# Half of the first-key indicator tiles built on ScalarE, and 12 gather steps moved in among the lead builds

## The reference, cut to what matters

```
q = (xb @ w_q).reshape(blk, 8, 2, 128)                     # 8 heads, 2 half queries
sc = einsum('thpd,hpnd->thpn', q, sub_keys)                # scores against 128 keys each
top_s, top_i = top_k(sc, 16)
cand_s = top_s[:, :, 0, :, None] + top_s[:, :, 1, None, :]
cand_i = top_i[:, :, 0, :, None] * 128 + top_i[:, :, 1, None, :]
best_s, sel = top_k(cand_s.reshape(blk, 8, 256), 16)
gate = softmax(best_s); idx = cand_i at sel                # 16 of 16384 experts per head
act = gelu(einsum('thkd,td->thk', exp_u[idx], xb))
out = einsum('thk,thkd->td', gate * act, exp_v[idx])
```

## Time and profile before

| | |
|---|---|
| median of 3 runs | 3154.22 us |
| the profiled execution | 3153.1 us |
| its span | 3151.3 us |
| PE busy | 2943.6 us (93%) |
| DVE busy | 2475.3 us (79%) |
| ACT busy | 813.6 us (26%) |
| POOL busy | 1019.5 us (32%) |
| HBM read | 1033.28 MB |
| mean granted TensorE clock | 0.95 |

### The profile page before, as it was taken

How to read it: one execution, slowest core, us unless ns; L and a number is a source line. 1 busy time by engine, 2 the same in 40 slices (tenths; PEclk the granted TensorE clock), 3 DMA queues, 4 the chain that set the end, 5 groups by cost and what they waited for, 6 DMA issues and landing times.

```text
span 3151.3 us, 46747 instructions
## 1 busy us (share of the span) xinstructions
PE 2943.6 (93%) x17342; PEld 2573.4 (82%) x17342; DVE 2475.3 (79%) x5415; ACT 813.6 (26%) x2398; POOL 1019.5 (32%) x840
## 2 busy tenths in 40 slices
PE   8898999999999999987888979989999999999977
PEld 7797788988888888875766957779888888888865
DVE  2368899988888888887654787998888888888878
ACT  5332222221111212211355353222221122211212
POOL 5433222322233332333365321222333333333322
PEclk9799999999999999999988978989999999999989
DMA  5237788899999999999521356778999999999997
GB/s 185 83 100 294 271 316 321 341 421 422 422 421 422 421 415 420 421 407 419 222 80 54 100 201 266 285 298 307 420 422 421 422 421 420 421 416 417 412 422 292
DMA packets 159967, 1042.99 MB, mean 331 GB/s; under 512 B 18480, under 2 KB 23920, under 8 KB 44096
## 3 DMA queue, kind: packets, MB, share of 16 engines
q0 software_dynamic: 92160, 671.13, 52.2%
q1 hardware_dynamic: 63648, 357.59, 29.1%
q10 hardware_dynamic: 4000, 12.36, 1.0%
HBM read 1033.28 MB, written 7.86 MB: 330 GB/s over the span
## 4 chain that ended last, share of the span: by engine, by line
DMA 44%; PE 28%; DVE 18%; issue 8%; ACT 2%; DVEq 0%; POOL 0%; ACTq 0%; POOLq 0%
DMA gata<-uvg,idxg 37%; DVE acc L1657 8%; DMA gatb<-uvg,idxg 7%; PE bank L519 6%; PE bank L720 6%; PE bank L506 3%; PE bank L508 3%; PE bank L507 3%; PE bank L707 2%; DVE gata L1649 2%; PE bank L536 1%; PE bank L607 1%; PE bank L586 1%; DVE oneA L1623 1%; DVE rstd L1396 1%
## 5 line engine op out<-in xcount | busy, mean ns | idle before, releaser
L733 PE MATMUL bank<-a,V 128*128 128x256 f32 x4096 | 928.5, 386 | 59.9 <-DVE a L1640 47.1
L720 PE MATMUL bank<-xd,U 128*128 128x256 f32 x4096 | 939.1, 389 | 2.2 <-DMA U<-uvd 2.2
L733 PEld LDWEIGHTS bank<-a,V 128*128 128x128 f32 x4096 | 791.7, 194 | 180.2 <-issue 50.4
L1309 POOL DMA_INDIRECT gata<-uvg,idxg x428 | 499.0, 1166 | 1251.7 <-DVE acc L1657 1196.1
L720 PEld LDWEIGHTS bank<-xd,U 128*128 128x128 f32 x4096 | 789.7, 195 | 110.3 <-DMA U<-uvd 3.0
L1649 DVE CUSTOM_DVE_ANT_0 gata<-gata,xrow 128x1024 f32<-128x1024 f32 x428 | 522.1, 1220 | 219.5 <-DMA gata<-uvg,idxg 213.7
L1103 ACT ACTIVATE act<-dot 128x1 f32<-128x1 f32 x640 | 129.5, 202 | 1666.6 <-DVE dot L1649 1666.5
L1657 DVE SCALAR_TENSOR_TENSOR acc<-gata,wgt,acc 128x1024 f32<-128x1024 f32 x428 | 547.5, 1279 | 1.6 <-ACT wgt L1105 1.4
L1309 POOL DMA_INDIRECT gatb<-uvg,idxg x212 | 246.4, 1162 | 533.0 <-DVE acc L1657 523.3
L1649 DVE CUSTOM_DVE_ANT_0 gatb<-gatb,xrow 128x1024 f32<-128x1024 f32 x212 | 258.5, 1220 | 110.0 <-DMA gatb<-uvg,idxg 108.1
L707 PEld LDWEIGHTS bank<-B,oneA 128*128 128x128 f16 x4096 | 279.1, 150 | 29.1 <-issue 13.8
(11 more groups left out here) (198 smaller groups left out, 2519.0 us busy)
## 6 DMA issues: line engine op xcount, KB each, us to landing
U<-uvd SPq DMA_DIRECT2D x128, 1024.0 KB
V<-uvd SPq DMA_DIRECT2D x128, 1024.0 KB
raw<-lin SPq DMA_DIRECT2D x152, 512.0 KB
gata<-uvg,idxg POOLq DMA_INDIRECT x428
hsp<-h ACTq DMA_DIRECT2D x2, 2304.0 KB, 14.0
hx<-hsp SPq DMA_DIRECT2D x2, 2304.0 KB, 16.6
gatb<-uvg,idxg POOLq DMA_INDIRECT x212
sk_g<-skT ACTq DMA_DIRECT2D x2, 1024.0 KB, 4.8
```

The lines of the kernel that those rows point to most:

```text
L720: mm = pe.matmul(bank[s][:, TD * t:TD * t + TD], U[:, s, o:o + P], xd[:, k, :], start=(t == 0 and k == 0), stop=(k == DT - 1), skip_group_ ...
L733: mm = pe.matmul(bank[b][:, TD * (d % 2):TD * (d % 2) + TD], V[:, s, o:o + P], a[:, s, TD * k:TD * k + TD], start=(first and k == 0 and d ...
L1309: pool.indirect_dma_start(row(l, s), None, uvg[l], bass.IndirectOffsetOnAxis(idxg[:, s:s + 1], 0)).then_inc(g_in[s % SLOTS], 16)
```

## The change

Three things are changed.

First, ScalarE makes one of the two halves of oneA for the 17 lead builds, the second 8 tokens of each build. It takes for each token the absolute distance between the key numbers and the token's first key (a bias operand holds minus the key, one number per partition), 8 instructions of 128 elements with a stride, and then one instruction of 1024 elements, 1 - distance clipped at zero. VectorE makes only the first half for these builds; for later builds nothing changes.

Second, `gates_high` also writes minus the first keys, one more ScalarE instruction for each of two token chunks, ahead of the semaphore that VectorE's `take` waits for.

Third, the number of steps at the places of the lead rises: in layer 0 two at every place but those with m % 4 == 1 (30 steps, 8 more), in layer 1 two at every even m (26, 4 more). The tail then has 39 steps in layer 0 and 42 in layer 1.

```
-     ("sel3", 3), ("sel4", 3), *[(f"hot{m}", 1 + (m % 4 == 0)) for m in range(LEAD)]],
+     ("sel3", 3), ("sel4", 3), *[(f"hot{m}", 1 + (m % 4 != 1)) for m in range(LEAD)]],
...
-     ("sel2", 3), ("sel3", 3), ("sel4", 3), *[(f"hot{m}", 1 + (m % 4 == 0)) for m in range(LEAD)]])
+     ("sel2", 3), ("sel3", 3), ("sel4", 3), *[(f"hot{m}", 1 + (m % 2 == 0)) for m in range(LEAD)]])
...
-            def build(l, m, s):
+            def build(l, m, s, lead=False):
...
+                if lead:
+                    pe.wait_ge(a_act, LEAD * l + m + 1)
...
-                act.activation(gh[...], bank[b][:, 0:TCS[c]], ACT.Copy,
-                               scale=GS).then_inc(gh_done, 1)
+                act.activation(gh[...], bank[b][:, 0:TCS[c]], ACT.Copy, scale=GS)
+                act.activation(minus1[...], bank[b][:, P:P + TCS[c]], ACT.Copy,
+                               scale=-1.0).then_inc(gh_done, 1)
+
+            def ones_half(l, m):
+                s, t0 = m % 2, TB * (m % (TD // TB)) + TG
+                half = oneA[:, s, 1]
+                for t in range(TG):
+                    ins = act.activation(half[:, :, t], iotaA[:, :, t], ACT.Abs,
+                                         bias=minus1[:, t0 + t:t0 + t + 1])
+                ins.then_inc(a_dist, 1)
+                act.wait_ge(a_dist, LEAD * l + m + 1)
+                act.activation(half, half, ACT.Relu, bias=1.0, scale=-1.0).then_inc(a_act, 1)
...
                 n = max(n, RING0 - 1)
+                act.wait_ge(iota_in, 16)
+                act.wait_ge(gh_done, len(DC) * (l + 1))
+                ones_half(l, 0)
+                ones_half(l, 1)
                 weights_at(l, "hot0")
                 for m in range(1, LEAD):
                     weights_at(l, f"hot{m}")
                     to_w(l, m - 1)
+                    if m + 1 < LEAD:
+                        ones_half(l, m + 1)
                     if m % 2 == 1 and n + m // 2 < RING - 1:
                         gelu(l, n + m // 2)
...
-                for u in range(TB // TG):
+                for u in range(1 if m < LEAD else TB // TG):
                     ins = dve.tensor_tensor(oneA[:, s, u], iotaA[:, :, :], ...
```

More of the change, by code:

```diff
@@ L186, in program @@
         rstd = at_("rstd", 205312, [P, T], F32)
+        minus1 = at_("minus1", 205312, [P, TD], F32)
         ident = at_("ident", 207616, [P, P], F32)
@@ L292, in program @@
         a_one, b_eq, b_one = sem("a_one"), sem("b_eq"), sem("b_one")
+        a_dist, a_act = sem("a_dist"), sem("a_act")
         a_done, sums_done, hsum_done, dsum_done = (sem(n) for n in ("a_done", "sums_done", "hsum_done", "dsum_done"))
@@ L757, in experts @@
                 for m in range(LEAD):
-                    build(l, m, m % 2)
+                    build(l, m, m % 2, lead=True)
                     if m % 2 == 0 and n + m // 2 < RING:
@@ L1071, in gates_high @@
                 act.wait_ge(full[b], BASE[f"gt{l}"][b] + 1)
-                act.activation(gh[:, TCO[c]:TCO[c] + TCS[c]], bank[b][:, 0:TCS[c]], ACT.Copy,
-                               scale=GS).then_inc(gh_done, 1)
+                act.activation(gh[:, TCO[c]:TCO[c] + TCS[c]], bank[b][:, 0:TCS[c]], ACT.Copy, scale=GS)
+                act.activation(minus1[:, TCO[c]:TCO[c] + TCS[c]], bank[b][:, P:P + TCS[c]], ACT.Copy,
+                               scale=-1.0).then_inc(gh_done, 1)
[3 more added lines that the diff above has]
+                for t in range(TG):
+                    ins = act.activation(half[:, :, t], iotaA[:, :, t], ACT.Abs, bias=minus1[:, t0 + t:t0 + t + 1])
+                ins.then_inc(a_dist, 1)
+                act.wait_ge(a_dist, LEAD * l + m + 1)
+                act.activation(half, half, ACT.Relu, bias=1.0, scale=-1.0).then_inc(a_act, 1)
             def gate_exp(l, n):
```

## The result

| | before | changed |
|---|---|---|
| median of the runs, us | 3153.64 (4 runs, 3150.38 to 3160.45) | 3185.33 (4 runs, 3182.45 to 3193.81) |
| span of the profiled execution, us | 3151.3 | 3183.9 |
| mean granted clock | 0.95 | 0.944 |

The change makes the kernel slower: the ratio of the times is 1.0099, 95% interval 1.008 to 1.0119. The forecast was 3138.5 us; the time lies above its range of 3126 to 3158 us too.

The account below looks back on a forecast made before the run. It took PE to bound the loop and leads, bytes the tails, V's turnaround close behind. -26 + 2.5 + 0.5 + 6 + 0.5 + 1 = -15.5 us on 3153.1 gave 3137.6, predicted median 3138.5 us, range 3126 to 3158.

Parts of the forecast that it names:

- The tail loses steps: Tails: eight steps fewer in layer 0, four in layer 1, gaining 17 and 9 us, together 26 us.
- the second limit named: Tail: turnaround of V, close behind the bytes, 8.5 to 9.3 us an iteration, 136 to 149 us for 16.
- VectorE in the lead: Lead: 1.64 us left per build; four builds with 7 steps take 22.9 us, within PE's 23.9.
- ScalarE's half tile: Lead builds: eight short instructions at 0.31 us and a long one of 1.05, together 3.6 us, ends 2.8 and 4.2.
- The added wait and the start: Leads: builds wait for ScalarE, 2.5 and 0.5 us; late starts, 6 us in layer 0, 0.5 in layer 1.
- the chain through both engines: Lead: last dot, weight, `to_w`, half tile, 4.5 us before the next build; some 1.5 us more a pair if ScalarE bounds.
- DMA in the lead: Leads: layer 0 rises to 388 GB/s, layer 1 to some 355; fits on average, 1 us for missed bursts, bounds 0 and 5.
- The rival in which ScalarE becomes the bound: Leads: at 5.0 us a half tile, pairs take 13.3 us plus some 1.5, total 3180 us; chance 0.14.
- The point from which it decides the sign: Half tile price turning gain to loss: about 4.9 us without the chain's part, about 4.2 with it in full.
- The table loads: Rival: each lead build has two loads of 1.28 us on ScalarE, 72 us in all, about 3210 us; chance 0.03.

Follow-up runs that it names:

- dense_more: dense_early with four more steps in each lead (34 in layer 0, 30 in layer 1): 3127.88 us, 0.9914 of the kernel before.
- dense_half: Changed kernel with ScalarE's half tile laid out token by token, short instructions reading and writing adjacent numbers: 3122.9 us, 0.9899 of before; second series 3131.15 us, 0.9927.
- steps_only: Kernel before with only the 12 moved steps, VectorE making both halves of every tile: 3133.93 us, 0.9933 of before.
- write_dense: Changed kernel with the eight short instructions writing adjacent numbers, still reading with the 16-byte stride (second 8 tokens' indicator wrong): 3142.95 us, one run.
- dense_early: dense_half with the first two half tiles of a lead ahead of the still open gelu: 3122.37 us, 0.9908 of before; again 3123.7 us, 0.9896.
- write_gap4: Changed kernel with the eight short instructions writing every second 2-byte number, a 4-byte stride (second 8 tokens' indicator misordered): 3136.52 us, one run.
- half_only: Changed kernel with the steps back at their old places, ScalarE's half tile alone: 3202.5 us, 1.0148 of the kernel before.

## Why the prediction was wrong

**The tail loses steps.** Right in layer 0, little over half in layer 1. Forecast -17 and -9 us; measured -16.0 and -5.0, plus 3.9 us between the layers that the forecast did not count: layer 0's last steps end after its last sums, and fewer steps end sooner. VectorE's last two axpys there, before and changed:

```profile
1531.74 2.67 DVE L1657 SCALAR_TENSOR_TENSOR acc<-gata,wgt,acc 128x1024 f32<-128x1024 f32 x2
```

```profile
1544.44 2.67 DVE L1678 SCALAR_TENSOR_TENSOR acc<-gata,wgt,acc 128x1024 f32<-128x1024 f32 x2
```

From the last piece of scores to its end pass 168.7 us before and 149.4 changed: 19.3 of the 20 us that eight steps are by bytes, with DMA at 419 GB/s. So the bytes still set the pace there up to the last step. For the sums the second limit named, the wait for V, came forward. PE's waits in that tail, two rows before and the one row changed:

```profile
PE bank L733 <- DVE a L1640: 22.2, 9, 5.1
PE bank L733 <- DMA V<-uvd: 8.9, 3, 3.2
```

```profile
PE bank L737 <- DMA V<-uvd: 19.9, 8, 5.4
```

That V's turnaround bounds a tail by itself is shown by dense_more alone, where DMA falls to 385 GB/s. In layer 1 four steps by bytes are 10 us; dense_half and steps_only also had only 6 of them there. DMA is no longer full (403 GB/s), and PE waits 17.3 us for the gate product and 7.8 for V; why not more was gained was not settled.

**VectorE in the lead.** Right. A build is 1.64 us with one half (506.66 to 508.33 in the changed kernel's trace is 1.67), and in dense_half, where ScalarE keeps up, layer 0's lead is 97.5 us with 30 steps, as long as before with 22 (97.3). With both halves on VectorE the steps cost 8.6 us (steps_only), where the prediction had 6.4.

**ScalarE's half tile.** This is the step that failed. The sum took 3.6 us, with bounds of 2.8 and 4.2; measured 6.0. The row with a bias operand was the right one for the instruction but not for its addresses: it reads and writes adjacent 4-byte numbers. dense_half, with adjacent addresses, has 3.5 us. The prediction did name "strided 2-byte writes at half rate" and about 5 us, but outside its bounds and with no row. Against it it put `to_w`, as a strided write at 0.59 us. That was misread: in the lead `to_w` reads its bank with a stride (128 bytes) and writes its 512 4-byte numbers side by side (`Wr[:, i, :, :, :]`), so its row says nothing of strided writes.

**The added wait and the start.** PE did wait for ScalarE's half tile, as named, and the size followed the half tile. With 6.0 us a pair needs 2 x 6.0 + 3.3 = 15.3 us of ScalarE by the prediction's own count, measured 14.8 to 15.2. The extra 1.5 us a pair for the chain through both engines, which the prediction added on top, did not come with it; nor did its 2.5 and 0.5 us with dense_half, whose leads are 0.3 us longer and 2.3 us shorter than before. Build 0 of layer 0 was 6.7 us later (4.3 forecast), with the half tile of 3.5 us 4.8; the scores behind it took 9.02 us in place of 7.14 (1.5 us more were forecast). Build 0 of layer 1 was 2.5 us later, where 0.5 was forecast: ScalarE begins its half tile at 2104.87, 1.1 us behind the turn, and at 3.6 us the delay would be about nothing. In dense_half it is still 2.0 us late, since the half tile begins 3.1 us behind the turn, after a weight that waits for its dot and the copy of the key numbers (0.43 us).

**DMA in the lead.** Not reached with the change (302 GB/s). In dense_half the lead moved 380 GB/s with no longer lead, as forecast (388).

**The sum and the rivals.** The rival in which ScalarE becomes the bound came true. It was priced at 3180 us for 5.0 us a half tile, and given 0.14; the time is 3185 at 6.0. That the two are close is luck: by its own working 6.0 us would give 3212 us, and 3188 without the 1.5 us a pair for the chain, which did not come. The point from which it decides the sign (4.2 to 4.9 us) is in keeping with write_dense: 4.5 us a half tile, leads of 103.9 and 101.2, and a total still under the kernel before. Where its assumption on the half tile held, in dense_half, the sign and rough size came out: 3138.5 forecast, 3122.9 and 3131.15 measured, better by 7 to 16 us. In the traced execution (3130.87 us) the gain is 22.2 us against 15.5 forecast. The tails give 20.8 us in place of 26, the starts cost 6.8 (6.5 forecast), and the leads beyond them are 2.0 us shorter where 4 us of cost were forecast. What the sum left out gives 6.2 more: 4.0 between the layers and 4.1 ahead of the first lead and after the last tail, less 1.9 in the loops. The table loads did not appear: before and changed have 49 each, and abs and relu ran between gelus with none in the leads, as the Trainium skill, "ScalarE: Activation LUTs", section "Table sets: the hidden batching unit", says.

The same page's rule (section "Rules for kernel authors") that relu belongs on VectorE was right about the change: steps_only, which follows it, is 51 us faster in the medians. It is not borne out with the adjacent layout: dense_half is 11 us faster than steps_only in their comparison, and the lead of layer 0 with its start is 3.5 us shorter (4.8 later, 8.3 less), since in steps_only VectorE is the bound of that lead and ScalarE has the room. How much of the total it is worth stays open: dense_half's second series (0.9927 of before) lies beside steps_only's 0.9933, while dense_early's (0.9896, at most 0.9911) lies below it.

## What to carry to other kernels

When work goes to an idle engine, price it from a row that matches in addresses and element size, not only in operation and count; without such a row, keep the slow end inside the range and ask from which price the sign turns. Before giving up such a change, try the layout: the same work with adjacent addresses turned a loss of 1.0% into a gain of 0.7 to 1.0%. And try each half of a change alone: most of that gain, 0.7%, came from the moved steps with every tile left on VectorE. And moving transfers out of a full stretch pays only until the next limit behind it, here the two buffers of V at 141 to 142 us.

## What was not expected of the hardware

- ScalarE's 128-element activations from 2-byte to 2-byte numbers: 0.30 us from start to start with all addresses adjacent, 0.44 with the read 16 bytes apart, 0.62 with the write 16 bytes apart (whatever the read), 0.44 with the write 4 bytes apart and 0.46 with 4-byte numbers written 16 bytes apart, both with the read 16 bytes apart.
- A mean duration can mislead where instructions overlap: 1061 ns each, at 0.62 us from one start to the next.
- Equal work took different times. The turn ahead of layer 0's lead, before which nothing differs, ended at 479.5 us in write_gap4 and at 487.4 in half_only. In the window from 100 to 200 us the kernel before (shown first; half_only has the same 0.88) and write_gap4 had granted clocks of 0.88 and 0.97:

```profile
100.00:200.00 100.00, 92.23 (x552) 83.92 (x553) 46.54 (x197) 36.61 (x69) 48.28 (x28) 0.88 0.31 97
```

```profile
100.00:200.00 100.00, 92.57 (x600) 85.18 (x601) 51.43 (x238) 39.96 (x77) 53.46 (x30) 0.97 0.34 105
```

So a difference of 8 us or less between two single runs says little, while a stage between two marks can be read closer.
